# When the heads of a two-map attention get their root-mean-square norm: at each head's end, or at the stream's end

## The reference, cut to what matters

```
probs = joint_softmax(*logits)
outs  = (p[:, 0] - lam * p[:, 1]) @ v          # two maps, one value matrix, 128 wide
o     = sum of outs over the key parts
diff_out = rmsnorm_2(o, subln_g) * (1.0 - lam_init)     # per token and head, over 128 values
y     = concatenate([oa, diff_out]) @ w_out
```

## Time and profile before

| | |
|---|---|
| median of 3 runs | 3999.74 us |
| lowest and highest | 3988.47 and 4002.08 us |
| the profiled execution | 4001.47 us |
| its span, first to last instruction | 3999.7 us |
| PE busy over the span | 3786.9 us (95%) |
| DVE busy over the span | 2063.7 us (52%) |
| granted TensorE clock, mean | 0.97 of full speed |

### The profile page before, as it was taken

One profiled execution on the slowest core, in us unless ns is written; L12 is line 12 of the kernel. 1 busy time (PEld: TensorE's weight loads), 2 busy tenths in 40 slices (PEclk: granted clock), 3 DMA queues, 4 the chain that ended last, 5 costly groups with the idle time before them and its releaser, 6 DMA issues. The chain is left out here.

```text
span 3999.7 us, 49029 instructions
## 1 busy us (share of the span) xinstructions
PE 3786.9 (95%) x19420; PEld 3183.6 (80%) x19420; DVE 2063.7 (52%) x3416; ACT 1287.0 (32%) x2149; POOL 1203.3 (30%) x548
## 2 busy tenths in 40 slices
PE   8999998999999998899989998899999889999999
PEld 6777776888777787688867777799999778877887
DVE  5547646565644773565456665623343566633112
ACT  4332244222433323422234443311111335543223
POOL 2224433444322443244421111122222210123443
PEclk8999999999999999999999997999999999999999
DMA  3224422333212442233321101233332200112332
GB/s 105 64 59 135 125 77 66 116 100 103 82 56 65 126 133 74 74 106 100 111 73 38 28 26 38 69 95 111 95 108 88 62 19 16 28 48 75 94 95 84
DMA packets 544449, 316.71 MB, mean 79 GB/s; under 512 B 35876, under 2 KB 517215, under 8 KB 544223
## 3 DMA queue, kind: packets, MB, share of 16 engines
q1 hardware_dynamic: 525184, 277.39, 23.9%
q10 hardware_dynamic: 19039, 36.19, 2.9%
HBM read 311.44 MB, written 2.10 MB: 78 GB/s over the span
## 5 line engine op out<-in xcount | busy, mean ns | idle before, releaser
L459 POOL TENSOR_TENSOR wlo<-wraw,whi 128x1024 fp32r<-128x1024 f32 (+6 forms) x544 | 1203.1, 2216 | 2774.9 <-ACT whi L452 2774.6
L475 PE MATMUL acc<-hh,whi 128*128 128x512 f32 (+2 forms) x2744 | 1064.1, 388 | 32.1 <-DVE hl L635 24.5
L476 PE MATMUL acc<-hl,whi 128*128 128x512 f32 (+2 forms) x2744 | 1034.7, 377 | 0.0
L477 PE MATMUL acc<-hh,wlo 128*128 128x512 f32 (+2 forms) x2744 | 1034.2, 377 | 0.0
L452 ACT ACTIVATE whi<-wraw 128x1024 fp32r<-128x1024 f32 (+6 forms) x544 | 523.7, 965 | 652.2 <-DMA wraw<-in_w_up 184.9
L475 PEld LDWEIGHTS acc<-hh,whi 128*128 128x128 f32 x2744 | 521.8, 190 | 146.8 <-issue 31.2
L476 PEld LDWEIGHTS acc<-hl,whi 128*128 128x128 f32 x2744 | 521.8, 190 | 91.5 <-issue 12.3
L477 PEld LDWEIGHTS acc<-hh,wlo 128*128 128x128 f32 x2744 | 521.0, 190 | 83.9
L1543 DVE TENSOR_TENSOR t<-acc,sq 128x768 f32<-128x768 f32 (+1 forms) x44 | 36.3, 825 | 444.3 <-PE acc L477 444.3
L475 PE MATMUL ob<-hh,whi 128*128 128x512 f32 (+3 forms) x576 | 214.3, 372 | 6.8 <-DVEq L831 6.6
L475 PE MATMUL acc<-act1h,whi 128*128 128x512 f32 x528 | 209.7, 397 | 1.4 <-DVE act1l L1551 1.4
(11 more groups left out here) (412 smaller groups left out, 6232.4 us busy)
## 6 DMA issues: line engine op xcount, KB each, us to landing
wraw<-in_ffn_w SPq DMA_DIRECT2D x120, 512.0 KB, 3.8
wraw<-in_w_in SPq DMA_DIRECT2D x102, 512.0 KB, 3.9
wraw<-in_w_up SPq DMA_DIRECT2D x88, 512.0 KB, 3.8
ada_w<-in_ada_w ACTq DMA_DIRECT2D x64, 512.0 KB, 4.1
ada_w<-in_ada_w SPq DMA_DIRECT2D x32, 512.0 KB, 4.2
wraw<-in_w_down SPq DMA_DIRECT2D x32, 512.0 KB, 4.0
wraw<-in_w_out SPq DMA_DIRECT2D x16, 512.0 KB, 4.1
wraw<-in_w_mkv SPq DMA_DIRECT2D x16, 512.0 KB, 4.0
```

The source lines that it names most:

```text
L459: e.tensor_tensor(wlo[0:rows, s, a:b, 0:w], wraw[0:rows, s, a:b, 0:w], whi[0:rows, s, a:b, 0:w].bitcast(F32), ALU.subtract).then_inc(lo_re ...
L475: e.matmul(o, wh, xh, start=first, stop=False)
L476: e.matmul(o, wh, xl, start=False, stop=False)
L477: return e.matmul(o, wl, xh, start=False, stop=last)
```

## The change

ACT roots six columns at a time, at the ends of iterations 6, 24, 42 and 60: each is the iteration in which DVE has written the last sum of a head. DVE multiplies two row blocks at the end of each of three iterations, 8, 9 and 10 for head 0, 26 to 28 for head 1, 44 to 46 for head 2 and 62 to 64 for head 3. The number of multiplies (24) and their form stay. The semaphore `subn_ready` now counts heads, and DVE waits for it at the first multiply of each head. PE's program, all transfers, and SP's and GpSimd's work are the same.

```
-        def normed_ab(e, c, t):
-            if t == 0:
-                e.wait_ge(subn_ready, 1)
-            for r in range(6):
+        def normed_ab(e, c, t, rows):
+            if rows[0] == 0:
+                e.wait_ge(subn_ready, t + 1)
+            for r in rows:
                 o = ot2[:, r, (4 + t) * P:(5 + t) * P]
                 e.scalar_tensor_tensor(out=o, in0=o, scalar=hss[:, t * 6 + r:t * 6 + r + 1], in1=subg[:, :], ...
...
-            def heads_rooted():
-                act.wait_ge(ss_ready, 1)
-                act.activation(hss[:, :], hss[:, :], ACT.Ln, ...).then_inc(act_step, 1)
+            def head_rooted(t):
+                ss = hss[:, 6 * t:6 * t + 6]
+                act.wait_ge(ss_ready, t + 1)
+                act.activation(ss, ss, ACT.Ln, ...).then_inc(act_step, 1)
                 act.wait_ge(act_step, c.next(act_step))
-                act.activation(hss[:, :], hss[:, :], ACT.Exp, scale=-0.5).then_inc(subn_ready, 1)
+                act.activation(ss, ss, ACT.Exp, scale=-0.5).then_inc(subn_ready, 1)
-            act_flow(..., hooks={60: heads_rooted})
+            act_flow(..., hooks={6: lambda: head_rooted(0), 24: lambda: head_rooted(1), 42: ..., 60: lambda: head_rooted(3)})
...
-            at_end = {60: lambda: dve.sem_inc(ss_ready, 1), 61: lambda: normed_ab(dve, c, 0), ..., 64: lambda: normed_ab(dve, c, 3)}
+            heads_end = {}
+            for t in range(4):
+                heads_end[18 * t + 6] = lambda: dve.sem_inc(ss_ready, 1)
+                for i in range(3):
+                    heads_end[18 * t + 8 + i] = lambda t=t, i=i: normed_ab(dve, c, t, (2 * i, 2 * i + 1))
```

More of the change, by code:

```diff
@@ L2268, in _ @@
             act.wait_ge(neg_ready, 1)
-            def heads_rooted():
-                act.wait_ge(ss_ready, 1)
-                act.activation(hss[:, :], hss[:, :], ACT.Ln, bias=small[:, 63:64], scale=1.0 / P).then_inc(act_step, 1)
+            def head_rooted(t):
+                ss = hss[:, 6 * t:6 * t + 6]
+                act.wait_ge(ss_ready, t + 1)
+                act.activation(ss, ss, ACT.Ln, bias=small[:, 63:64], scale=1.0 / P).then_inc(act_step, 1)
                 act.wait_ge(act_step, c.next(act_step))
-                act.activation(hss[:, :], hss[:, :], ACT.Exp, scale=-0.5).then_inc(subn_ready, 1)
-            act_flow(act, c, its_ab(), jobs_ab(), ticks_ab(), hooks={60: heads_rooted})
+                act.activation(ss, ss, ACT.Exp, scale=-0.5).then_inc(subn_ready, 1)
+            act_flow(act, c, its_ab(), jobs_ab(), ticks_ab(),
+                     hooks={6: lambda: head_rooted(0), 24: lambda: head_rooted(1), 42: lambda: head_rooted(2), 60: lambda: head_rooted(3)})
             act_features(act, c, hh, LAST_FEATURES, 6)
@@ L2483, in _ @@
             dve.sem_inc(neg_ready, 1)
-            at_end = {60: lambda: dve.sem_inc(ss_ready, 1), 61: lambda: normed_ab(dve, c, 0), 62: lambda: normed_ab(dve, c, 1),
-                      63: lambda: normed_ab(dve, c, 2), 64: lambda: normed_ab(dve, c, 3)}
-            dve_flow(dve, c, its_ab(), jobs_ab(), ticks_ab(), hooks=at_end)
+            heads_end = {}
[3 more added lines that the diff above has]
+                    heads_end[18 * t + 8 + i] = lambda t=t, i=i: normed_ab(dve, c, t, (2 * i, 2 * i + 1))
+            dve_flow(dve, c, its_ab(), jobs_ab(), ticks_ab(), hooks=heads_end)
             dve_features(dve, c, hh, hl, LAST_FEATURES, 6)
```

## The result

The changed kernel took 4004.7 us, the median of 22 runs, beside 3999.2 us for the kernel before in as many runs on the same chips. The ratio is 1.0017, with a 95% interval of [1.0010, 1.0023]: 4 to 9 us slower, and by the bound of 0.3% no change. Timed again beside other kernels it came out at 1.0004 [0.9995, 1.0013].

What follows compares the result with a forecast made beforehand. PE, busy 95% of the span, was taken as the bound, with a DVE and ACT loop pacing the tail. Heads +5.7, tail -4.3, roots nothing: +1.4 us, 4002.9 on the profiled execution, 4001 us as median; range 3990 to 4010 us.

Steps and rivals of the forecast that it cites:

- What the tail gives back: Tail: fewer multiplies on the DVE and ACT loop give 4.5 us, taken as 4.3; bounds 2.5 and 8.5 us.
- What the roots cost: ACT at heads' ends: three earlier Ln and Exp pairs, 0.54 us each, hide in 3.06 us idle; cost nothing.
- What the heads cost: Head places of heads 0 to 2: multiplies delay maxima, 1.9 us per head, 5.7 in all; bounds nothing to 4.0 us.
- the two pairs that it named: Ends of iterations 8 and 9: the first delays PE 0.53 us, both together 1.9 us; iteration 10's pair costs nothing.
- the hold: End of iteration 9: multiplies wait for GpSimd's low-half instruction, ending about 0.4 us behind it; PE then 1.9 us late, iteration 8 included.
- The rule that spoke against the change: DVE instructions with two SBUF inputs share a locked read port with GpSimd: 1.9 us per head, against 0.9 without.
- The sum: Whole kernel: 5.7 - 4.3 = +1.4 us on the profiled execution, 4002.9 us; as a median 4001 us, no change.
- the rival on the head places: PE's clock falls behind the new stall before the scores of 12, some 3 us per head, 4010 us; chance 0.12.
- the rivals: Heads hide it, 3995.4 to 3998 us (0.21); tail clock rises, 3997 (0.14); head clock falls, 4010 (0.12); not as said, 4006 (0.02).
- A sign that I named for being wrong: Head places or tail: granted clock differing from before's by more than a few hundredths would show the prediction wrong.
- The two stretches: Stream's start to head 3's last sum 5 to 6 us more; from there to the stream's end 4 to 4.5 less.
- the step that leaves the clock unchanged: Whole stream: the sum, 5.7 - 4.3 us, counts only head and tail delays, with no term for the clock.

Runs made afterwards that it cites:

- e5: Kernel before with only the roots taken at each head's end as in the changed kernel, all 24 multiplies still in the tail; ratio to before 0.9999.
- e2: Changed kernel with the middle pair of heads 0 to 2 moved from the end of iteration 9 to 11, away from GpSimd; ratio to before 0.9989.
- e8: Changed kernel with GpSimd writing zeros instead of subtracting in the three head places, so three weight tiles lack a low half; ratio to before 0.9983.
- after again: The changed kernel, unaltered, timed again with a second profile; stream 334.89 us, ratio to before 1.0004.
- e4: Changed kernel's head places plus all 24 multiplies in the tail as before, so heads 0 to 2 are normed twice; ratio to before 1.0030.
- e1: Changed kernel with the multiply pairs of heads 0 to 2 at the ends of iterations 7, 10 and 11; ratio to before 0.9991.
- e3: Changed kernel with the multiplies of heads 0 to 2 left out, head 3's and the roots kept; ratio to before 0.9995.

## Why the prediction was right, and where it was not

**What the tail gives back.** Right: 4.54 us in the maxima, where the working gave 4.5 and I took 4.3. PE did not become the pace; it still waited 1.06 us for ACT.

**What the roots cost.** Right: nothing that shows, by e5 (heads 0 and 2 to 0.03 us).

**What the heads cost.** Right: 1.84 to 1.87 us where I said 1.9, by the two pairs that it named. With e2 and e8 the parts stand alone: about 0.5 us for the pair at iteration 8, 1.3 for the hold. The pair took 1.91 us beside GpSimd's subtraction and 0.61 without it. The rule that spoke against the change (the Trainium skill, SBUF — State Buffer, section "Who interferes with whom") agrees with that.

**The sum.** Measured, 3 heads give 5.56 us and the tail takes 4.54: +1.0, forecast +1.4. But the streams differ by 4.9. The other 3.9 us are clock, which the sum put at nothing and left to a rival of 0.12; they come in two parts.

The first is the rival on the head places. I gave "the head places lose the clock" 0.12, and 3 us in each of three heads. It came in head 0 as described, behind the 1.30 us stall, and cost 1.6 us: 3.4 us at half the speed cost about half of that. The prediction said "the next 6 us of PE work" at twice their time and then 3 us, which doesn't fit: 6 us of work would cost 6 us, and 3 us is what 6 us of time at half the speed cost. Head 1 had the same stall, 1.31 us, and kept its clock. In head 2 the clock fell ahead of the scores, behind waits of 0.77 and 0.29 us, as the 1-us windows of the kernel after show:

```profile
2356.00:2357.00 1.00, 0.81 (x8) 0.57 (x7) 0.42 (x1) 0.37 (x2) 0.83 (x1) 1.00 1.09 330
2357.00:2358.00 1.00, 0.90 (x3) 0.75 (x4) 0.95 (x1) 0.00 (x0) 1.00 (x1) 0.68 0.31 92
2358.00:2359.00 1.00, 1.00 (x4) 0.81 (x3) 1.00 (x3) 0.00 (x0) 0.53 (x1) 0.50 0.00 0
```

PE's slower projection filled the time in which it would have stood: its wait before the scores was 0.23 us instead of 1.30, and the fall cost nothing. So the rival held in place and sign, but not in size: 1.6 us in one head, nothing in the two others, where it said 9 us in all. The falls in these places stand in the three profiles with the held pair (after, after again, e4) and in none of the nine without it. That the stall itself brings them down is not shown: head 1 speaks against it, and head 2's came first.

The second part, about 2.3 us, comes from low stretches at heads' ends: 1.6 us each in the windowed parts of heads 1 and 2 and 0.3 in the sums, less 1.2 in the tail. The one at head 1's end is not the change's. PE waits 2.00 and 1.9 us there in before too. Windows at head 1's end, first of the kernel before, then of the kernel after:

```profile
2246.00:2249.00 3.00, 1.11 (x9) 1.11 (x10) 2.22 (x10) 1.89 (x6) 0.00 (x0) 1.00 0.01 3
```

```profile
2249.00:2252.00 3.00, 1.52 (x7) 1.52 (x8) 1.75 (x8) 1.95 (x6) 0.00 (x0) 0.50 0.01 3
2252.00:2255.00 3.00, 3.00 (x9) 2.01 (x7) 0.40 (x3) 1.37 (x6) 0.00 (x0) 0.51 0.00 0
```

With the same work the clock held in one execution and fell in the other, and it fell here in every other profile of the study, before's second one among them (0.50, behind the same wait of 2.01 us). The Trainium skill (TensorE: Matmul & The Clock Gate, section "What's actually happening") has activity lift the clock, and says that the point at which the level changes varies between runs of one kernel. The trace agrees with the latter: the kernel before had 1.00 here in one profile and 0.50 in the other. What decides it in a given execution is left open.

The one at head 2's end is another matter. Its 1.6 us in the windowed part of head 2 stand in the three profiles with the held pair alone. In the nine others that part takes 59.0 to 59.6 us, but for 60.57 in before's second profile, whose low stretch lies elsewhere. So of the 3.9 us of clock 3.2, in head 0's place and at head 2's end, go with the held pair. The other 0.7 is 1.6 at head 1's end and 0.3 in the sums, less 1.2 in the tail; e1 and e3, which have the changed tail and no held pair, show about as much: they are 3.4 and 3.5 us shorter than before where the order alone gives 4.5, so 1.1 us of clock. Whether the stall brings these falls, or the later time at which the stream comes to the place, no run here tells apart.

**The verdict.** No change by the bound, as forecast, and 4001 us is 3.7 below the median; the range held it, which owes something to luck: the range was drawn from the rivals and the runs' spread, and the sum behind 4001 us had no term for the clock. A sign that I named for being wrong did show: the clock in head 0's place was 0.68 where before had 1.00, and the tail's differed by 0.13. The two stretches also came out otherwise than said, both by the clock: 10.6 us more up to head 3's last sum, for 5 to 6, and 5.8 us less behind it, for 4 to 4.5. So the account of the order on DVE was right, and the step that leaves the clock unchanged was not.

## What to carry to other kernels

Work that is moved to an idle engine has to be placed by what stands behind it in that engine's queue and, as here, by what GpSimd does in that microsecond: by the order alone the same 18 multiplies cost 0, 0.5 or 1.9 us per head in three sets of places a few microseconds apart. Look for the wait inside the loop that the work is already in before moving it elsewhere; here DVE's wait for ACT ahead of the low half took all of it. A change of a few microseconds is read from stretches of the trace, and one profile's clock is checked against a second profile of the same program before a difference is put down to the change.

## What the hardware showed that was not expected

The low clock can hide a stall as well as make one: in head 2, 3.4 us at half speed cost nothing, since PE had 1.3 us to wait anyway. And the tail of the same program ran 2.9 us shorter in a second profile (52.24 for 55.15), with the multiplies in it 5.51 us apart in both. So the loop kept its pace at either level. The difference lies ahead of the first multiply, 1.45 us, where PE ran at 1.2 GHz in the first profile and at 2.4 in the second, and behind the last group, 1.46 us.
